# Two operand tensors of TensorE placed elsewhere in SBUF: chunks 16 bytes further apart, and a tensor behind the arena

## Chip, cores, metric

One core of one Trainium2 chip runs the whole program. The metric is the device time of one execution in microseconds (us), the median of several; lower is better.

## What is computed

Two transformer blocks, one behind the other, on 256 tokens of width 1024, all in float32. The first block has two layers, each with a SwiGLU, an attention (sliding window with sinks beside a latent attention in layer 0, forgetting attention in layer 1), a second SwiGLU and a gated projection. The second block merges a block attention with a gated spatial mix, attends to a memory of 256 rows, and ends in a retrieval layer over 16,384 experts. Cut to the two parts that bear on the change:

```python
def swiglu(x, w_gate_up, w_down):                 # four times, 1024 -> 2816 -> 1024
    g, u = jnp.split(x @ w_gate_up, 2, axis=-1)
    return (jax.nn.silu(g) * u) @ w_down
...
def peer_ffn(h, w_q, subkeys, w_down, w_up):      # once, 16384 experts
    ...
    a = jax.nn.gelu(jnp.einsum("td,thkd->thk", xc, w_down[e]))
    return jnp.einsum("thk,thkd->td", g * a, w_up[e])
```

## The kernel before

Tokens are in two tiles of 128 (`NT`), the width in eight chunks of 128 (`KC`). Weights stream from HBM in units of 1 MB (`raw`, a ring of three units, each of four blocks of 512 columns). Full float32 accuracy comes from a split: ScalarE rounds a unit to float32r (`w_hi`, line 276) and VectorE keeps the rest (`w_lo`, line 281). The activations are split in the same way, and both halves stand side by side: `x_both` is [128 partitions, 8 chunks, 2 halves, 256 tokens], `a_both` the same with 4 chunks. The views `x_hi`, `x_lo`, `a_hi`, `a_lo` are its halves.

Each product is three matmuls of float32r. There are two ways in which they stand:

- `product` (lines 321, 322, 325) serves all dense layers and the way down in the retrieval layer. The stationary operand, loaded by LDWEIGHTS, is 128 tokens of one chunk of `x_both` or `a_both`; the moving operand is a block of 512 columns of `w_hi` or `w_lo`. `product_part` (lines 2550 to 2552) does the same at the very end, in part with 256 columns.
- `wide_pair` (lines 2177 and 2180) serves the queries and the way up in the retrieval layer. Here the stationary operand is 128 columns of the weights, and the moving operand is a whole chunk of `x_both` or `a_both`, both halves in one run of 512 elements (line 2177), or its first half alone (line 2180). Two chunks go together: two matmuls of 512 columns, then two of 256, called a four below.

```python
for k in (k0, k0 + 1):
    pe.matmul(out[:, :], w_hi[:, s, b, at:at + P], source(k).rearrange("p s t -> p (s t)"), ...)
for k in (k0, k0 + 1):
    last = pe.matmul(out[:, 0:T], w_lo[:, s, b, at:at + P], source(k)[:, 0, :], ...)
```

In the queries `source(k)` is `x_both` for all eight k. In the experts it is `wide_both` (line 2149): chunks 0 to 3 of `x_both`, then the four of `a_both`. A third user is the forget gate (lines 1429 to 1434): its stationary operand is `f_both`, of 32 or 16 columns, its moving operand 256 columns of `x_both`.

ScalarE and VectorE write both tensors: lines 350 and 360 (a chunk at a time), and lines 2530 and 2537 (two chunks in one instruction). Every engine's order is written out by hand, with semaphores between them; nothing in it depends on an address.

**Places.** SBUF tensors lie in a partition in the order in which they are created, each start rounded up to 32 bytes. In the built program `w_hi` starts at byte 41,088 and takes 24,576 bytes, then come `w_lo`, `h` (90,240), `x_both` (98,432), `a_both` (114,816), `mid` (123,008), `gated`, the small tensors, `one_i` (137,664), `f_both` (150,464) and `arena` (152,128, 69,632 bytes). From `w_hi` to `x_both` it is 57,344 bytes, 28 times 2,048, and a chunk of `x_both` or `a_both`, a block of `w_hi` or `w_lo` and a half of `mid` each have 2,048 bytes. So each of these starts a whole number of times 2,048 bytes from `w_hi`, and each 128 columns a multiple of 512 bytes: this is called the grid below. `f_both` (109,376 bytes from `w_hi`) and `arena` (111,040) are off it, by 320 and 448 bytes over a multiple of 512.

Of the kernel before, what the change touches and what calls it, by code (L numbers as in the profile page):

```python
# [7 lines left out]
F32R = mybir.dt.float32r  # L8
# [9 lines left out]
T, D = 256, 1024  # L18
NT, KC = T // P, D // P
# [17 lines left out]
EC = 4  # L37
# [4 lines left out]
EV_WIDTHS = (384, 384, 416)  # L42
EV_COLS = (0, 384, 768, 1184)
BLOCK = 32

# [98 lines left out]
def build(nc, a, stop=None):  # L146
    with ExitStack() as ctx:
        def sb(name, cols, dt=F32):
            return ctx.enter_context(nc.sbuf_tensor(name, [P] + list(cols), dt))
# [22 lines left out]
        raw = sb("raw", [RING, UB, BLK])  # L172
        w_hi, w_lo = sb("w_hi", [RING, UB, BLK], F32R), sb("w_lo", [RING, UB, BLK], F32R)
        h = sb("h", [NT, D])
        x_both, a_both = sb("x_both", [KC, 2, T], F32R), sb("a_both", [EC, 2, T], F32R)
        x_hi, x_lo = x_both[:, :, 0, :], x_both[:, :, 1, :]
        a_hi, a_lo = a_both[:, :, 0, :], a_both[:, :, 1, :]
        mid = sb("mid", [NT, BLK])
        gated = sb("gated", [EC, T])
        gains, consts = sb("gains_sb", [N_GAINS]), sb("consts_sb", [N_CONSTS])  # L180
# [4 lines left out]
        f_hi, f_lo = f_both[:, :, 0, :], f_both[:, :, 1, :]  # L185
        stat = sb("stat", [5, 2 * HEADS_C])
        arena = sb("arena", [17408])
        banks = ctx.enter_context(nc.psum_tensor("banks", [P, 8, BLK], F32))
        bank = [banks[:, b, :] for b in range(8)]
        ACC, BACK = (0, 1, 2, 3), 6  # L190
# [461 lines left out]
        def vector_back(dve, key, c, quarters):  # L652

            b = c % 2
            for q in quarters:
                if q == 0:
                    dve.wait_ge(*dve_done["mid", key, c, 1])
                rows = slice(q * BLOCK, (q + 1) * BLOCK)
                src = mid[rows, :, b * FC:(b + 1) * FC].rearrange("p t (f o j) -> p t f o j", f=2, j=BLOCK)
                for o in range(P // BLOCK):  # L660
                    dst = turned[o * BLOCK:(o + 1) * BLOCK, b, :, :].rearrange("p f (t o i) -> p t f o i", t=NT, i=BLOCK)
                    last = dve.transpose(dst[:, :, :, q, :], src[:, :, :, o, :])  # L662
# [2333 lines left out]
```

## Time and profile before

| | |
|---|---|
| runs | 2036.25, 2036.39, 2036.99 us, median 2036.39 |
| span of the profiled execution | 2034.3 us |
| its own time | not listed beside the span; the median is 2.1 us above the span |
| TensorE (matmuls) busy | 2021.4 us, 99% |
| weight loads busy | 1698.9 us, 84%, beside the matmuls |
| VectorE, ScalarE, GpSimd busy | 1545.4, 1076.5, 23.3 us |
| bytes moved by DMA | 433.76 MB, mean 213 GB/s |

The span is the time from the first instruction to the last in one profiled execution. A matmul's record is longer than the distance to the next one, because matmuls overlap in the array; what a matmul costs is the distance from its start to the start of the next.

### The profile page before, as it was taken

How to read it: one execution, taken by the hardware profiler on the slowest of the kernel's cores; microseconds unless marked ns; L12 is line 12 of the kernel's file. 1: busy time of each engine (PE TensorE's matmuls, PEld its weight loads, DVE VectorE, ACT ScalarE, POOL GpSimd, SP SyncE). 2: the span in 40 equal slices, each digit the busy share in tenths (PEclk: the TensorE clock that was granted, in tenths of full speed). 3: DMA queues.
4: the chain of work that ended last, by engine and by line, in shares of the span. 5: the costliest groups of instructions: out<-in, count | busy, mean ns of one | idle time of the engine just before them, and what ended most of it. 6: DMA issues, size and time to landing. Idle time of an engine off the chain costs nothing.

```text
span 2034.3 us, 26355 instructions
## 1 busy us (share of the span) xinstructions
PE 2021.4 (99%) x10387; PEld 1698.9 (84%) x10387; DVE 1545.4 (76%) x2466; ACT 1076.5 (53%) x1332; POOL 23.3 (1%) x38
## 2 busy tenths in 40 slices
PE   9999999999999999999999999999999999999998
PEld 7888788888888887888888888888888888888887
DVE  7886778876977566887676756999989857677675
ACT  6445664446444556444557556556566654444443
POOL 0000000000000000000000000000000000000000
PEclk9999999999999999999999999999999999999999
DMA  7654345554555442555554535466799998777773
GB/s 266 226 197 168 137 163 192 201 189 168 206 189 204 149 162 110 202 191 189 189 207 148 184 126 206 161 234 230 236 293 287 298 333 319 305 303 280 281 287 114
DMA packets 97033, 433.76 MB, mean 213 GB/s; under 512 B 7728, under 2 KB 41152, under 8 KB 52496
## 3 DMA queue, kind: packets, MB, share of 16 engines
q1 hardware_dynamic: 95584, 426.51, 59.0%
q0 software_dynamic: 1328, 5.58, 0.8%
q8 instruction: 83, 1.36, 0.3%
q14 instruction: 38, 0.31, 0.0%
HBM read 397.46 MB, written 34.60 MB: 212 GB/s over the span
## 4 chain that ended last, share of the span: by engine, by line
PE 96%; DVE 2%; ACT 1%; issue 0%; DMA 0%; SPq 0%; POOLq 0%; POOL 0%; DVEq 0%; ACTq 0%
PE banks L321 23%; PE banks L325 23%; PE banks L322 23%; PE banks L2177 13%; PE banks L2180 7%; PE banks L328 3%; PE banks L2400 1%; PE banks L981 1%; PE banks L1016 1%; DVE w_lo L281 1%; DVE arena L662 0%; PE banks L507 0%; PE banks L2240 0%; DMA raw<-in_w 0%; PE banks L406 0%
## 5 line engine op out<-in xcount | busy, mean ns | idle before, releaser
L281 DVE TENSOR_TENSOR w_lo<-raw,w_hi 128x2048 fp32r<-128x2048 f32 x334 | 763.9, 2290 | 269.7 <-ACT w_hi L276 268.0
L276 ACT ACTIVATE w_hi<-raw 128x2048 fp32r<-128x2048 f32 x335 | 640.4, 1914 | 471.6 <-PE banks L325 457.0
L321 PE MATMUL banks<-w_hi,x_both 128*128 128x512 f32 (+2 forms) x1488 | 581.0, 390 | 0.4 <-DVE mid L743 0.2
L325 PE MATMUL banks<-w_hi,x_both 128*128 128x512 f32 (+2 forms) x1488 | 577.0, 388 | 0.0
L322 PE MATMUL banks<-w_lo,x_both 128*128 128x512 f32 (+2 forms) x1488 | 576.8, 388 | 0.0
L321 PEld LDWEIGHTS banks<-w_hi,x_both 128*128 128x128 f32 x1488 | 279.3, 188 | 58.1 <-issue 1.1
L325 PEld LDWEIGHTS banks<-w_hi,x_both 128*128 128x128 f32 x1488 | 279.3, 188 | 56.9
L322 PEld LDWEIGHTS banks<-w_lo,x_both 128*128 128x128 f32 x1488 | 279.5, 188 | 54.8
L321 PE MATMUL banks<-w_hi,a_both 128*128 128x512 f32 x608 | 239.8, 394 | 0.3 <-DVE a_both L1103 0.2
L325 PE MATMUL banks<-w_hi,a_both 128*128 128x512 f32 x608 | 236.8, 390 | 0.0
L322 PE MATMUL banks<-w_lo,a_both 128*128 128x512 f32 x608 | 236.8, 389 | 0.0
L2177 PE MATMUL banks<-x_both,w_hi 128*128 128x512 f32 x640 | 203.7, 400 | 0.0
L662 DVE STREAM_TRANSPOSE arena<-mid 32x128 f32<-32x128 f32 x640 | 193.5, 302 | 9.1
L2177 PE MATMUL banks<-a_both,w_hi 128*128 128x512 f32 x512 | 160.8, 395 | 0.0
L2180 PEld LDWEIGHTS banks<-x_both,w_lo 128*128 128x128 f32 x640 | 120.2, 188 | 28.4
L321 PEld LDWEIGHTS banks<-w_hi,a_both 128*128 128x128 f32 x608 | 114.1, 188 | 25.1 <-issue 1.5
L325 PEld LDWEIGHTS banks<-w_hi,a_both 128*128 128x128 f32 x608 | 114.1, 188 | 24.2
L322 PEld LDWEIGHTS banks<-w_lo,a_both 128*128 128x128 f32 x608 | 114.2, 188 | 22.6
L2180 PE MATMUL banks<-x_both,w_lo 128*128 128x256 f32 x640 | 126.0, 278 | 0.0
L2180 PEld LDWEIGHTS banks<-a_both,w_lo 128*128 128x128 f32 x512 | 96.2, 188 | 22.7
L2180 PE MATMUL banks<-a_both,w_lo 128*128 128x256 f32 x512 | 100.6, 278 | 0.0
L2177 PEld LDWEIGHTS banks<-x_both,w_hi 128*128 128x128 f32 x640 | 97.4, 189 | 0.1
(238 smaller groups left out, 1669.7 us busy)
## 6 DMA issues: line engine op xcount, KB each, us to landing
raw<-in_w SPq DMA_DIRECT2D x337, 1024.0 KB, 4.8
parked_t<-arena SPq DMA_DIRECT2D x32, 512.0 KB, 9.6
arena<-parked_t SPq DMA_DIRECT2D x8, 2048.0 KB, 10.5
arena<-parked_a SPq DMA_DIRECT2D x32, 512.0 KB, 5.9
parked_a<-one_i SPq DMA_DIRECT2D x21, 512.0 KB, 7.6
parked_a<-mid SPq DMA_DIRECT2D x11, 512.0 KB, 8.1
raw<-in_w SPq DMA_DIRECT2D x12, 256.0 KB, 7.1
one_i<-in_alibi POOLq DMA_DIRECT2D x1, 1024.0 KB, 6.1
```

The source lines that it names most:

```text
L276: act.activation(w_hi[:, u % RING, :, :], raw[:, u % RING, :, :], ACT.Copy).then_inc(*act_done.mark("w_hi", u))
L281: e.tensor_tensor(w_lo[:, u % RING, :, :], raw[:, u % RING, :, :], f32(w_hi[:, u % RING, :, :]), ALU.subtract).then_inc(*dve_done.mark("w_ ...
L321: pe.matmul(out, hi, w_hi[:, s, b, 0:width], start=start, stop=False)
L322: pe.matmul(out, hi, w_lo[:, s, b, 0:width], start=False, stop=False)
L325: return pe.matmul(out, lo, w_hi[:, s, b, 0:width], start=False, stop=stop)
L328: return pe.transpose(out, src, ident[0:src.shape[0], 0:src.shape[0]])
L662: last = dve.transpose(dst[:, :, :, q, :], src[:, :, :, o, :])
L981: last = pe.matmul(bank[b][:, j * nk:(j + 1) * nk], self.q(h0 + j, n), self.k(h0 + j)[:, k0:k0 + nk], start=True, stop=not self.masks)
L1016: last = pe.matmul(out, self.v(rh + j, tiles[i]), self.ext_at(r)[:, (j * len(tiles) + i) * P:(j * len(tiles) + i + 1) * P], start=i == 0, ...
L2177: pe.matmul(out[:, :], w_hi[:, s, b, at:at + P], source(k).rearrange("p s t -> p (s t)"), start=k == 0, stop=False)
L2180: last = pe.matmul(out[:, 0:T], w_lo[:, s, b, at:at + P], source(k)[:, 0, :], start=False, stop=k == KC - 1)
L2400: last = pe.matmul(bank[banks[j // 4]][:, j % 4 * P:(j % 4 + 1) * P], hot_i[:, slot, j // 2, :, j % 2], hot_j[:, slot, 1 + k, j // 2, :, j ...
```

## The change

`x_both` becomes a view of a tensor with rows of 516 elements, of which 512 are used, so a chunk starts 2,064 bytes behind the last one instead of 2,048. `a_both` is created last, behind `arena`. Nothing else is changed: on all five engines the same instructions stand in the same order, with the same shapes.

```diff
+APART = 4
...
-        x_both, a_both = sb("x_both", [KC, 2, T], F32R), sb("a_both", [EC, 2, T], F32R)
-        x_hi, x_lo = x_both[:, :, 0, :], x_both[:, :, 1, :]
-        a_hi, a_lo = a_both[:, :, 0, :], a_both[:, :, 1, :]
+        x_rows = sb("x_both", [KC, 2 * T + APART], F32R)
+        x_both = x_rows[:, :, 0:2 * T].rearrange("p k (s t) -> p k s t", s=2)
...
         arena = sb("arena", [17408])
+        a_both = sb("a_both", [EC, 2, T], F32R)
+        x_hi, x_lo = x_both[:, :, 0, :], x_both[:, :, 1, :]
+        a_hi, a_lo = a_both[:, :, 0, :], a_both[:, :, 1, :]
```

In the built program `x_both` still starts at 98,432; its chunk k is 16 k bytes off the grid. `a_both` starts at 213,696, which is 172,608 bytes from `w_hi`, 576 more than a multiple of 2,048 (64 more than one of 512). All that lies between, from `mid` to `arena`, moves down by 8,192 bytes less 128.

## Rows read from the trace of the kernel before

**Rows 1.** The page: busy time, and the chain that ended last, by engine and line.

```profile
PE 2021.4 (99%) x10387; PEld 1698.9 (84%) x10387; DVE 1545.4 (76%) x2466; ACT 1076.5 (53%) x1332; POOL 23.3 (1%) x38
...
PE 96%; DVE 2%; ACT 1%; issue 0%; DMA 0%; SPq 0%; POOLq 0%; POOL 0%; DVEq 0%; ACTq 0%
```

**Rows 2.** Span and mean granted TensorE clock of the core; PE's waits for DMA.

```profile
core 0: 2034.3 us, clock 0.999
...
PE banks L328 <- DMA consts_sb<-in_consts: 2.8, 1, 2.8
```

**Rows 3.** The page: groups by line; count, busy us, mean ns of a record.

```profile
L321 PE MATMUL banks<-w_hi,x_both 128*128 128x512 f32 (+2 forms) x1488 | 581.0, 390 | 0.4 <-DVE mid L743 0.2
...
L321 PE MATMUL banks<-w_hi,a_both 128*128 128x512 f32 x608 | 239.8, 394 | 0.3 <-DVE a_both L1103 0.2
...
L2177 PE MATMUL banks<-x_both,w_hi 128*128 128x512 f32 x640 | 203.7, 400 | 0.0
...
L2177 PE MATMUL banks<-a_both,w_hi 128*128 128x512 f32 x512 | 160.8, 395 | 0.0
```

**Rows 4.** Timeline of PE in a dense layer: start us, length us, instruction.

```profile
499.66 0.39 PE L321 MATMUL banks<-w_hi,x_both 128*128 128x512 f32 x1
...
511.90 0.39 PE L321 MATMUL banks<-w_hi,x_both 128*128 128x512 f32 x1
```

**Rows 5.** Timeline of PE, experts: fours of chunks 2-3, 4-5, 6-7, 0-1.

```profile
1500.31 0.63 PE L2177 MATMUL banks<-x_both,w_hi 128*128 128x512 f32 x2
1500.78 0.40 PE L2180 MATMUL banks<-x_both,w_lo 128*128 128x256 f32 x2
1501.01 0.63 PE L2177 MATMUL banks<-a_both,w_hi 128*128 128x512 f32 x2
1501.48 0.39 PE L2180 MATMUL banks<-a_both,w_lo 128*128 128x256 f32 x2
...
1502.17 0.40 PE L2180 MATMUL banks<-a_both,w_lo 128*128 128x256 f32 x2
1502.40 0.63 PE L2177 MATMUL banks<-x_both,w_hi 128*128 128x512 f32 x2
1502.87 0.39 PE L2180 MATMUL banks<-x_both,w_lo 128*128 128x256 f32 x2
...
1504.49 0.63 PE L2177 MATMUL banks<-a_both,w_hi 128*128 128x512 f32 x2
```

**Rows 6.** Timeline of PE, queries: second matmul pairs of chunks 0-1 and 2-3.

```profile
1271.81 0.40 PE L2180 MATMUL banks<-x_both,w_lo 128*128 128x256 f32 x2
...
1272.51 0.39 PE L2180 MATMUL banks<-x_both,w_lo 128*128 128x256 f32 x2
```

**Rows 7.** Timeline of PE, last unit: 256 columns, stationary 128 columns.

```profile
2025.97 0.28 PE L2551 MATMUL banks<-w_lo,x_both 128*128 128x256 f32 x1
...
2027.89 0.28 PE L2552 MATMUL banks<-w_hi,x_both 128*128 128x256 f32 x1
```

**Rows 8.** Timeline of PE, forget gate: 256 columns, stationary 32 or 16 columns.

```profile
693.48 0.28 PE L1429 MATMUL banks<-x_both,f_both 128*32 128x256 f32 x1
...
694.61 0.28 PE L1434 MATMUL banks<-x_both,f_both 128*16 128x256 f32 x1
```

**Rows 9.** Timeline of PE, the unsplit product (plain float32): eight matmuls and the next.

```profile
223.83 3.60 PE L507 MATMUL banks<-raw,mid 128*128 128x512 f32 x8
227.26 0.38 PE L981 MATMUL banks<-arena 128*128 128x128 f32 x2
```

**Rows 10.** Weight loads by line: ns min/median/max, first and last start.

```profile
L321 PEld LDWEIGHTS banks<-w_hi,x_both x1488: 186/188/192, 19.2 to 2016.4; 128*128 128x128 f32 x186
...
L507 PEld LDWEIGHTS banks<-raw,mid x24: 188/190/192, 217.6 to 226.4; 128*128 128x128 f32 x24
...
L2240 PEld LDWEIGHTS banks<-arena x64: 187/192/192, 1260.2 to 1302.4; 128*128 128x128 f32 x64
```

**Rows 11.** Groups by form on ACT and DVE, on and off the grid: busy us, mean ns.

```profile
L2530 ACT ACTIVATE x_both<-gated 128x512 fp32r<-128x512 f32 x44 | 25.0, 615 | 0.0
...
L2490 ACT ACTIVATE mid<-banks 128x512 f32<-128x512 f32 x22 | 13.2, 598 | 50.9 <-PE banks L2180 50.9
L1038 ACT ACTIVATE arena<-banks 128x512 f32<-128x512 f32 x10 | 6.0, 597 | 6.8 <-PE banks L328 6.7
```

## The prediction

> **What bounds the kernel.** I read the page's busy times and its chain first: TensorE is busy for 99% of the span, and 96% of the chain that ended last is TensorE's own [rows 1]. Then the clock and PE's waits: it holds full speed (0.999), and its longest wait for a transfer is 2.8 us, once, at the start [rows 2]. So nothing but the pace of the matmuls counts, and that is read from distances between starts in PE's timeline, by kind of matmul, since no instruction is added, removed or moved.
>
> - Dense layers, moving weights, stationary tokens: from 499.66 to 511.90 us there are 54 steps, 226.7 ns each [rows 4]. At the full clock of 2.4 GHz 512 columns take 213.3 ns, so each matmul has 13.4 ns over its columns.
> - Wide fours, moving tokens, stationary weights: from 1500.31 to 1504.49 there are six fours [rows 5], 696.7 ns each. Two matmuls at 226.7 ns would leave 243.3 ns for the two of 256 columns.
> - 256 columns with a full stationary operand: 1.92 us over 16 steps, 120 ns each [rows 7], again 13.3 ns over the columns (106.7 ns). With a stationary operand of 32 or 16 columns it is 1.13 us over 10 steps, 113 ns [rows 8], 6.3 ns over.
> - Plain float32, which streams at half the pace: 3.43 us for eight, 428.8 ns each, 2.1 ns over twice 213.3 [rows 9].
>
> The surplus is thus the same for 512 and for 256 columns, and it shrinks with the stationary operand. It belongs to the weight load, not to the stream.
>
> **The change, part by part.** What changes is at which byte of a partition an operand starts. The question is if any duration depends on that.
>
> *Chunks of x_both, 16 bytes further apart.* They are stationary in 3 x 1488 matmuls of the dense kind and moving in 640 wide ones and as many of 256 columns [rows 3]. Chunk 0 keeps its distance to the weights, chunks 1 to 7 leave the grid by 16 to 112 bytes. Three readings say that the place does not matter. First, the dense distance is 226.7 ns through all chunks, both halves and both token tiles of the stretch, at all the distances between operands that occur. Second, the wide fours do have a small rhythm, and it does not go with the address: in the experts the pair of 256 columns on chunks 0-1 is recorded with 0.39 us and that on chunks 2-3 with 0.40 us, and so on in turn [rows 5], while in the queries, with the same chunks of x_both and the same places in the weight unit, chunks 0-1 have 0.40 us and chunks 2-3 have 0.39 us [rows 6]. If a distance of addresses set it, it could not change sides. It is a beat of the pipeline that starts anew behind each interruption. Third, f_both lies off the grid by 320 bytes over a multiple of 512, and its matmuls are the ones with the small surplus [rows 8]; the surplus per stationary column is no lower than on the grid (6.3 ns for at most 32 columns, 13.4 ns for 128), so that being off the grid neither freed it nor hurt it visibly.
>
> What no row shows is a full-pace stream whose stationary operand of 128 columns is off the grid, so this term is bounded from both sides. Upwards: weight loads on the grid take 190 ns (from mid), off it 192 ns (from arena), both of plain float32 [rows 10]; 2 ns for each affected matmul is the most that these rows allow. Downwards: the whole surplus over the best paced stream, 13.4 less 2.1, is 11.3 ns. I take 0, since the three readings are of the very instructions in question and the 2 ns are within the loads' own spread (188 to 192 ns from mid).
>
> *a_both behind the arena.* It is stationary in 3 x 608 dense matmuls and moving in 512 wide ones and 512 of 256 columns [rows 3], 2848 in all. In before it runs exactly as x_both does: its fours stand in the same 696.7 ns rhythm [rows 5]. Now it is 64 bytes over a multiple of 512 away from the weights. The bounds per matmul are the same, and I take 0 for the same reasons. That it is 98,880 bytes further up can't matter for a reason that a row shows: w_hi and w_lo are 24,576 bytes apart, and both feed the same 226.7 ns.
>
> *All from mid to arena moves down.* Transposes, attention, scatter and the tables keep their distances to each other; only those to the weights change. Transfers keep their rows and sizes, and PE waits for none of them after the start [rows 2].
>
> *ScalarE and VectorE.* The writes of two chunks at once now step by 2,064 bytes. The nearest rows: ScalarE's 128x512 copy from PSUM takes 598 ns into mid, on the grid, and 597 ns into arena, off it [rows 11]. Into x_both from gated it takes 615 ns. Even 10 ns more on these few dozen would be hidden: both engines have a quarter or more of the span idle, and the chain has 2% and 1% of them [rows 1]. Cost 0; should that cover go, 64 pairs of two at 10 ns are 1.3 us.
>
> The sum is 0. Against the profiled execution's span of 2034.3 us that is a span of 2034.3 us; the median of the runs shown stands 2.1 us above the span, and I forecast 2036.4 us.
>
> A rule on the pace stands against "0". The Trainium skill, page "TensorE: Matmul & The Clock Gate", section "Back-to-back issue gap", gives a warm distance of N/2.4 + 2.5 ns, which is 215.8 ns for 512 columns. The plain float32 row agrees with its surplus, the float32r rows are 10.9 ns above. If placement were what keeps them from it, the gain would be that of rival B. The same skill, page "SBUF — State Buffer", section "Who interferes with whom", gives PE two independent read ports, one for the moving operand and one for the weight load; by that the two could not disturb each other at any distance, and the sum would stay 0. No run here shows the ports.
>
> **The rivals.** A difference of 0.2%, 4.1 us, is about what a measurement of this kernel can tell from none.
>
> *A: only the wide fours get smoother.* If the skew lets the moving chunks stream without the extra beat, a four would go from 696.7 ns to 2 x 226.7 + 2 x 113 = 679.4 ns. There are (640 + 512) / 2 = 576 fours; 17.3 ns each is 10.0 us, to 2026.4 us. With the 120 ns of the last unit instead, a four would take 693.4 ns, and 576 x 3.3 ns = 1.9 us, no change that can be told. For it: these are the only matmuls with the touched tensors as moving operand, and they are slower than the dense ones. Against it: the beat changes sides between equal addresses [rows 5, 6].
>
> *B: weight read and stream collide on the grid.* Then the surplus of every matmul off the grid falls to 2.1 ns: (7/8 x 4464 + 1824) = 5730 x 11.3 ns = 64.7 us in the dense layers. Seven eighths of the 320 x_both fours and all 256 of a_both make 536, each going from 696.7 to 2 x 215.4 + 2 x 108.8 = 648.4 ns, 25.9 us. Together 90.6 us, to 1945.8 us. For it: the surplus exists, and goes with the size of the weight load and with the pace. Against it: f_both, already off the grid, still pays 6.3 ns for a quarter of the columns or less.
>
> *C: loads off the grid are longer, and that is not hidden.* The price is the 2 ns of arena over mid [rows 10]. On a_both's 2848 matmuls it is 5.7 us, to 2042.1 us; if chunks 1 to 7 of x_both pay too, 7/8 x (4464 + 1280) = 5026 more, 15.7 us in all, to 2052.1 us. It decides from the point where the matmul after the load has to start later for it. A load of 188 ns overlaps a distance of 226.7 ns, so a longer record need not show; but a fixed surplus that goes with the load suggests that part of it is on the path. From 1.4 ns on, on a_both alone, it could be told. Against it: 190 and 192 ns are medians within one spread.
>
> That the change doesn't do what it says can be left aside: the built program has the new addresses.
>
> **How the numbers follow.** No change: 0.71. A: 0.11, of which the small version falls under no change. B: 0.03, with 0.01 for some other gain. C: 0.14. So faster 0.15, same 0.71, slower 0.14. No change alone holds 2036.4 give or take 1.5 us and not 8 in 10. A and C's a_both case are about equally likely, so the range takes in both: 2026 to 2043 us. B and the full C stay out.
>
> **What would show it.** Right: 226.7 ns between dense matmuls on x_both and on a_both, 696.7 ns a four, 120 and 113 ns for the 256 columns, loads of 188 ns, TensorE busy within 2 us of 2021.4. A shows as a shorter distance in the fours with 226.7 ns unchanged; B as 215 ns in every dense layer but for chunk 0; C as 188 going to 190 or more on a_both and a distance grown by as much. A gain or loss in which no distance between matmuls has moved would prove my reading of the bound wrong.

## The result, and the profile after

The changed kernel takes 2069.43 us in the median (2068.88 to 2070.03, 4 runs) against 2036.56 us for the kernel before, measured with it (2036.25 to 2036.99). The ratio is 1.0161, with a 95% interval of 1.0149 to 1.0173: 32.9 us slower, outside the range given. The profiled execution took 2069.60 us, with a span of 2067.8 us; the same 1.8 to 2.1 us lie around the span.

The page after the change, busy times and the groups that answer to [rows 1, 3]; lines are three further down:

```profile
PE 2055.1 (99%) x10387; PEld 1703.3 (82%) x10387; DVE 1546.0 (75%) x2466; ACT 1077.4 (52%) x1332; POOL 23.2 (1%) x38
...
L324 PE MATMUL banks<-w_hi,x_both 128*128 128x512 f32 (+2 forms) x1488 | 588.0, 395 | 0.2
...
L324 PE MATMUL banks<-w_hi,a_both 128*128 128x512 f32 x608 | 243.6, 401 | 0.3 <-DVE a_both L1106 0.2
...
L2180 PE MATMUL banks<-x_both,w_hi 128*128 128x512 f32 x640 | 203.2, 398 | 0.0
...
L2180 PE MATMUL banks<-a_both,w_hi 128*128 128x512 f32 x512 | 159.8, 393 | 0.0
```

VectorE and ScalarE are busy for as long as before, to within 1 us, and no wait of PE grew: its busy time grew by 33.7 us. The mean records of the dense matmuls are 5 to 7 ns longer (390 to 395, 394 to 401), those of the wide ones are 2 ns shorter. PE's timeline in the same dense layer as [rows 4] (start us, length us):

```profile
500.18 0.40 PE L324 MATMUL banks<-w_hi,x_both 128*128 128x512 f32 x1
...
506.94 0.39 PE L328 MATMUL banks<-w_hi,x_both 128*128 128x512 f32 x1
```

These are 29 steps, 6.76 us, 233.1 ns each instead of 226.7 ns. Clock and waits are unchanged (answering [rows 2]), and so are the weight loads, 188 ns on either tensor (answering [rows 10]):

```profile
core 0: 2067.8 us, clock 1.000
```

```profile
PE banks L331 <- DMA consts_sb<-in_consts: 2.8, 1, 2.8
```

```profile
L324 PEld LDWEIGHTS banks<-w_hi,x_both x1488: 186/188/193, 20.5 to 2049.8; 128*128 128x128 f32 x186
L324 PEld LDWEIGHTS banks<-w_hi,a_both x608: 186/188/190, 42.7 to 2038.6; 128*128 128x128 f32 x152
```

Adding up the distances from each matmul's start to the next one's, in both traces, gives where the span's 33.5 us went:

| matmuls | before us | after us | difference |
|---|---|---|---|
| dense on x_both, 512 columns, x4320 | 985.8 | 1006.6 | +20.8 |
| first unit of the program, x48 | 11.2 | 12.2 | +1.0 |
| dense on a_both, x1824 | 417.9 | 428.7 | +10.8 |
| fours with x_both, x320 | 225.9 | 226.8 | +0.9 |
| fours with a_both, x256 | 178.4 | 177.8 | -0.6 |

That is 32.9 of 33.5 us, nearly all of it on the matmuls whose stationary operand was moved. Below, "distance" alone means this time from start to start; "off the grid by n" is the number of bytes between operand and streamed weights over a multiple of 256, the period that the runs gave. The theory going in (P): what counts is where the stationary operand lies in relation to the streamed one. The other letters (L, S, A0 and those that follow) name the rivals, each in the expectation where it first stands.

### The profile page after: what moved, and what is told of

It is laid out like the page before. It is cut to its first block, busy times and chain, and to the rows that moved or that the text cites. A ratio compares the mean times of both kernels' runs of the same rounds, so it can differ in the third digit from the quotient of the medians.

```text
span 2067.8 us, 26355 instructions
## 1 busy us (share of the span) xinstructions
PE 2055.1 (99%) x10387; PEld 1703.3 (82%) x10387; DVE 1546.0 (75%) x2466; ACT 1077.4 (52%) x1332; POOL 23.2 (1%) x38
## 4 chain that ended last, share of the span: by engine, by line
PE 98%; DVE 1%; ACT 0%; issue 0%; DMA 0%; SPq 0%; POOLq 0%; POOL 0%; DVEq 0%
PE banks L324 24%; PE banks L325 23%; PE banks L328 23%; PE banks L2180 13%; PE banks L2183 7%; PE banks L331 3%; PE banks L2403 1%; PE banks L984 1%; PE banks L1019 1%; PE banks L510 0%; PE banks L2243 0%; PE banks L409 0%; PE banks L412 0%; DMA h<-in_x 0%; PE banks L415 0%
## 5 line engine op out<-in xcount | busy, mean ns | idle before, releaser
L324 PE MATMUL banks<-w_hi,x_both 128*128 128x512 f32 (+2 forms) x1488 | 588.0, 395 | 0.2
L325 PE MATMUL banks<-w_lo,x_both 128*128 128x512 f32 (+2 forms) x1488 | 583.5, 392 | 0.0
L328 PE MATMUL banks<-w_hi,x_both 128*128 128x512 f32 (+2 forms) x1488 | 583.3, 392 | 0.0
L324 PE MATMUL banks<-w_hi,a_both 128*128 128x512 f32 x608 | 243.6, 401 | 0.3 <-DVE a_both L1106 0.2
L328 PE MATMUL banks<-w_hi,a_both 128*128 128x512 f32 x608 | 240.3, 395 | 0.0
```

The source lines that it names most:

```text
L324: pe.matmul(out, hi, w_hi[:, s, b, 0:width], start=start, stop=False)
L325: pe.matmul(out, hi, w_lo[:, s, b, 0:width], start=False, stop=False)
L328: return pe.matmul(out, lo, w_hi[:, s, b, 0:width], start=False, stop=stop)
```

## Each part alone, and the same parts on the grid

**Only the 16 bytes between chunks.**

```diff
         x_both = x_rows[:, :, 0:2 * T].rearrange("p k (s t) -> p k s t", s=2)
+        between = sb("between", [480])
+        a_both = sb("a_both", [EC, 2, T], F32R)
```

> Only the 16 bytes between the chunks of x_both; a_both stays behind x_both and on the grid (480 unused elements fill up to it). Theory P (what counts is the distance, to within a few hundred bytes, between the stationary operand that is being loaded and the columns that are streaming): the dense matmuls on x_both keep their longer distances (after: 7.3 + 7.2 + 6.4 us more on lines 321, 322, 325, 0.9 us in the first unit), those on a_both go back to 227 ns; about 22 us over before, 2059 us. Rival L (what hurts is that a_both lies far away, behind the arena, or beside nothing): the dense distances on x_both would be as before, 2036.5 us. Rival S (the step of 2,064 bytes hurts writes or multi-chunk operands and PE waits for them): 2059 us too, but with PE's dense distances at 227 ns and the loss in waits.

**Only a_both moved.** (`APART = 0`, and 128 unused bytes that keep a_both's byte.)

```diff
-APART = 4
+APART = 0
...
+        between = sb("between", [32])
```

> Only a_both behind the arena, at the same byte as in the change; x_both's chunks at 2,048 bytes again (128 unused bytes behind it). Theory P: dense distances on a_both 233 ns as in the change, on x_both 227 ns; the a_both part of the loss is 3.9 + 3.8 + 3.1 us dense less 0.6 us in the fours, so 2047 us. Rival L: the same on a_both. Together with the other part it should add up to the 33 us of the change if the two parts are independent.

**a_both behind the arena, on the grid.** The last kernel with 1,472 more unused bytes.

```diff
+        behind = sb("behind", [368])
         a_both = sb("a_both", [EC, 2, T], F32R)
```

> As the run with a_both alone moved, but 1,472 unused bytes ahead of a_both, so that it lies behind the arena and yet a whole number of times 2,048 bytes from w_hi. Theory P: all dense distances 227 ns, 2036.5 us, no change. Rival L (place far away): 233 ns on a_both as before this padding, 2047 us.

**All of the kernel before, 64 bytes later.**

```diff
+        ahead = sb("ahead", [16])
         raw = sb("raw", [RING, UB, BLK])
```

> The kernel before with 64 unused bytes ahead of everything, so every operand starts 64 bytes later, and all distances between operands are kept. Theory P: 227 ns everywhere, 2036.5 us. Rival A0 (the operand's own address counts, a start at 64 bytes over the old one is slow as a_both's is in the change): dense distances 233 ns on both tensors, some 35 us more, 2071 us.

Measured together, against 2036.81 us for the kernel before:

| kernel | us | ratio (95%) | dense distance on x_both, a_both |
|---|---|---|---|
| x_both's chunks apart | 2062.13 | 1.0126 (1.0109 to 1.0143) | 229.5 to 233.7 ns by chunk, 228.1 |
| a_both moved | 2051.16 | 1.0072 (1.0055 to 1.0088) | 227.3, 233.3 |
| a_both behind, on the grid | 2036.60 | 1.0000 (0.9990 to 1.0009) | 227.0, 227.1 |
| all shifted by 64 | 2036.63 | 0.9999 (0.9989 to 1.0009) | 227.0, 227.1 |

(Distances here are means from the starts in each trace, leaving out those over 300 ns; the kernel before has 227.0 and 227.2 by the same count.) The kernel with a_both moved, the one line by tensor, as ns min/median/max of a record:

```profile
L325 PE MATMUL banks<-w_hi,x_both x1488: 334/389/577, 20.3 to 2031.8; 128*128 128x512 f32 x180, 128*128 128x384 f32 x4, 128*128 128x416 f32 x2
...
L325 PE MATMUL banks<-w_hi,a_both x608: 393/398/504, 42.1 to 2020.9; 128*128 128x512 f32 x152
```

And the one with a_both behind the arena and on the grid:

```profile
L326 PE MATMUL banks<-w_hi,a_both x608: 389/389/504, 41.6 to 2005.9; 128*128 128x512 f32 x152
```

A record of 389 ns goes with a distance of 227 ns, 394 with 233 and 398 with 236. With a_both alone moved, the slow matmuls are those whose own operand was moved, and 1,472 bytes of padding take the whole loss on a_both away with the tensor still behind the arena. So it is neither the place nor the neighbourhood (L falls), and no start address in itself (A0 falls), but the relation between the operands. S falls too: no wait of PE grew.

A rival of another kind is that the moved operand meets the other engines' reads and writes of SBUF, or the transfers, and not PE's own stream. The trace of the kernel with a_both moved speaks against it. 39 of its dense matmuls on a_both ran, from 230 ns ahead of their start to the start of the next one, with no instruction on ScalarE, VectorE or GpSimd: 233.3 ns on average, as all of them. 408 ran with no DMA packet under way: 233.2 ns.

The two parts cost 25.3 and 14.4 us, 39.7 us in sum, against 32.9 us together. The missing 6.8 us lie in what each part does to matmuls that it does not touch: in the fours (with x_both apart alone, the fours on the untouched a_both take 702.6 ns instead of 697.1; with a_both moved alone, its own take 703.6 and x_both's 699.3; with both parts 694.7 on a_both; all of these without the 34 fours on x_both that stand behind an interruption) and in the dense ones on a_both next to skewed ones, 228.1 ns with x_both apart alone. So the time of a matmul depends on the matmuls around it too.

## Which distances are slow

Four kernels, one execution each, give the chunks of x_both 32 placements and a_both four. The edits are the step (`APART = 32`, then 4), an unused tensor ahead of x_both, and one between it and a_both.

> Chunks of x_both 128 bytes further apart (distances to the weights 0, 128, ... 896 bytes off the grid), a_both 256 bytes off the grid for all its chunks. Theory P with a short period (64 bytes or less would be contradicted already, since 64 is slow; a period of 128 bytes): 227 ns on all chunks, 2036.5 us. P with a period of 256: chunks 0, 2, 4, 6 and a_both at 227 ns, chunks 1, 3, 5, 7 slower, up to 235 ns, some 15 us in all. P with a period of 512: only chunks 0 and 4 at 227 ns, a_both slow too, some 30 us. Rival N (any distance off the grid is slow, however the distance): all but chunk 0 near 233 ns, over 35 us.

> x_both starts 128 bytes off the grid and steps by 16 (128 to 240), a_both 32 bytes off. With a period of 128 bytes the dense distances by chunk repeat those of the change: 229.5, 231, 232, 233, 234, 229.5, 234, 233 ns. With a longer period they differ. a_both: about 232 ns, as chunk 2 of x_both in the change.

> x_both 256 to 368 bytes off the grid in steps of 16, a_both 128 bytes off. With a period of 256 (or 128) bytes: as in the change by chunk, about 25 us over before. Otherwise the eight values show what the distance does, and whether any place is faster than the grid's 227 ns (by the surplus over the columns the most that could be had is 11 ns).

> x_both 384 to 496 bytes off the grid in steps of 16, a_both 448 bytes off (64 bytes short of a multiple of 512). Theory P says that only the distance counts; whether it is symmetric (448 like 64, so 233 ns) or whether a load that lies just ahead of the stream is better or worse is open. A place faster than 227 ns, if there is one, would be among these or the last runs' ones.

They took 2056.80, 2068.88, 2071.73 and 2064.51 us, beside 2036.64 us for the kernel before. Mean dense distance by bytes off the grid, from all kernels so far; where there are two numbers they are the least and the most of the chunks (of either tensor) at that place:

| bytes (mod 256) | 0 | 16 | 32 | 48 | 64 | 80 | 96 | 112 |
|---|---|---|---|---|---|---|---|---|
| ns | 227.0 | 231.0 to 231.1 | 231.6 to 233.4 | 232.6 to 232.8 | 233.0 to 233.4 | 230.4 to 230.9 | 233.7 to 233.8 | 232.3 to 232.6 |

| bytes (mod 256) | 128 | 144 | 160 | 176 | 192 | 208 | 224 | 240 |
|---|---|---|---|---|---|---|---|---|
| ns | 231.6 to 233.9 | 232.5 to 232.6 | 232.8 | 229.8 to 230.5 | 229.0 to 231.5 | 232.2 | 232.6 | 232.3 to 232.6 |

The 227.0 ns at 0 is that of kernels wholly on the grid. In the run with steps of 128 bytes a_both at 256 had 227.4 to 228.5 ns, chunks at 0, 256, 512 and 768 had 230.2 to 230.8 ns, and those at 128, 384, 640 and 896 had 231.6 to 233.5 ns: 128 is slow and 256 is not. The eight chunks at 256 to 368 bytes took what those at 0 to 112 took in the change to 0.4 ns, but for the first of them, 230.4 against 229.3 ns. So the period is 256 bytes, and an on-grid chunk between off-grid ones pays 2 to 4 ns for its neighbours. The rival of "any distance is alike" (N) falls with 80, 176 and 192. It falls most cleanly on a_both, whose chunks all lie alike: 233.0 ns at 32, 233.4 at 64, 233.2 at 128 and 229.2 at 448, that is 192. So it is not symmetric either. No chunk was faster than on the grid, though of the three matmuls of a product on a_both at 192 the first took 226.5 ns, the third 231.7.

**Steps of 256 bytes** (`APART = 64`, a_both right behind):

> Chunks of x_both 256 bytes further apart, a_both right behind on the grid. Theory P, with the period of 256 bytes that the scan gave: all dense distances 227 ns, 2036.5 us, no change, though no two chunks lie a multiple of 2,048 bytes apart. Rival Q (consecutive chunks must lie a whole number of 512, 1,024 or 2,048 bytes apart): some 15 us or more over before, at chunks 1, 3, 5, 7.

2036.77 against 2036.49 us, ratio 1.0001 (0.9992 to 1.0011), 226.8 to 227.3 ns for every chunk. So chunks may be as far apart as one likes in steps of 256 bytes, and Q falls.

**Steps of 4 bytes** (`APART = 1`):

> Chunks of x_both 4 bytes (one element) further apart, so chunk k lies 4 k bytes off the grid; a_both 32 bytes off. Theory P in the form that only whole 16-byte pieces count: chunks 0 to 3 as chunk 0 of the change (227 to 229.5 ns), chunks 4 to 7 as its chunk 1 (231 ns). If starting inside a 16-byte piece costs something of its own, chunks 1, 2, 3, 5, 6, 7 are slower than chunks 0 and 4. The matmuls on a_both: 233 ns, as at 32 bytes in the scan.

2069.30 us, in one execution. Chunks 0 to 7 had 230.8, 232.4, 231.7, 231.4, 231.9, 231.4, 231.5 and 233.7 ns, and a_both 233.2 ns, as expected. Four bytes off are already slow, in no order that whole 16-byte pieces would give, but chunk 0, on the grid, isn't at 227 ns in this company either. What starting inside a piece of 16 bytes costs by itself isn't told apart.

## Which pair of operands it is

**w_lo alone shifted.**

```diff
-        w_hi, w_lo = sb("w_hi", [RING, UB, BLK], F32R), sb("w_lo", [RING, UB, BLK], F32R)
+        w_hi = sb("w_hi", [RING, UB, BLK], F32R)
+        ahead = sb("ahead", [48])
+        w_lo = sb("w_lo", [RING, UB, BLK], F32R)
+        behind = sb("behind", [464])
```

> Placement of before, but w_lo 192 bytes further (64 short of a multiple of 256), so that the distance from w_lo to x_both and a_both is 64 bytes over the grid and that of w_hi is unchanged; 1,856 unused bytes behind w_lo keep the rest. Theory P: only the distances of line 322, which streams w_lo, go to 233 ns, lines 321 and 325 stay at 227 ns; 2048 matmuls by 6 ns, 12 us, 2049 us, give or take what the fours do. Rival X (the place of x_both or a_both against something other than the streamed weights, such as raw, h or consts): no change.

2048.12 us, in one execution as the next two: the total is as expected, its place is not. The distances on x_both are 229.4, 229.4 and 228.5 ns on lines 324, 325 and 328 (321, 322, 325 of before), not 227, 233 and 227. X, which had no change, falls.

**The halves of x_both 64 bytes apart.** The wide matmul takes its operand as two runs of 256.

```diff
-        x_both, a_both = sb("x_both", [KC, 2, T], F32R), sb("a_both", [EC, 2, T], F32R)
+        x_rows = sb("x_both", [KC, 2 * T + 64], F32R)
+        x_both = x_rows[:, :, 0:2 * T + 32].rearrange("p k (s t) -> p k s t", s=2)[:, :, :, 0:T]
+        a_both = sb("a_both", [EC, 2, T], F32R)
```

> In x_both the second half (x_lo) of each chunk starts 64 bytes later, chunks 2,304 bytes apart (on the 256-byte grid); a_both untouched. The wide matmul reads the two halves as two runs of 256. Line 322 loads x_lo's weights for line 325 while w_lo streams; line 325 itself then runs with x_lo as its stationary operand, while the next x_hi is loaded. Theory P (the load for the next matmul against the stream of this one): of the dense distances on x_both, line 322's go to about 233 ns, lines 321 and 325 stay near 227 ns. Rival O (the matmul's own stationary operand against its own stream): line 325's go to 233 ns, 321 and 322 stay. In both 1440 by 6 ns, 9 us, so some 2045 us.

2055.10 us. The three lines of `product` on x_both, ns min/median/max of a record:

```profile
L323 PE MATMUL banks<-w_hi,x_both x1488: 334/389/583, 20.1 to 2035.5; 128*128 128x512 f32 x180, 128*128 128x384 f32 x4, 128*128 128x416 f32 x2
...
L324 PE MATMUL banks<-w_lo,x_both x1488: 335/392/398, 20.3 to 2035.7; 128*128 128x512 f32 x180, 128*128 128x384 f32 x4, 128*128 128x416 f32 x2
...
L327 PE MATMUL banks<-w_hi,x_both x1488: 331/397/401, 20.5 to 2036.0; 128*128 128x512 f32 x180, 128*128 128x384 f32 x4, 128*128 128x416 f32 x2
```

The distances are 228.5, 229.2 and 235.4 ns. The largest part falls on the matmul with x_lo as its own stationary operand, where O has it, and not on the one beside whose stream x_lo is loaded. But the loss is 18.6 us, twice the 9 us that both P and O gave.

**Both low parts 64 bytes further**, so that x_lo is again in step with w_lo (the last edit, and 16 and 496 unused elements around w_lo):

> As the run with x_lo 64 bytes further, and w_lo 64 bytes further too. On x_both line 322 then streams w_lo (64) while it loads x_lo (64): distance 0; lines 321 and 325 stream w_hi (0) and load x_hi (0): distance 0. If the load for the next matmul against the present stream is what counts (P), all three are at 227 ns on x_both. If the matmul's own stationary operand against its own stream counts (O), line 322 (x_hi, w_lo) and line 325 (x_lo, w_hi) are both slow, 233 ns or more. If it is the step from one load to the next (or from one stream to the next) that counts (R), line 325 stays near 235 ns as in the last run. On a_both, which has no gap, line 322 loads on the grid against w_lo at 64: some 229 ns in all three, as in the run with w_lo shifted.

2065.82 us, and 232.1, 231.3 and 230.3 ns on x_both: all three are slow. P in its narrow form (only load against present stream) would have 227 ns three times, O 227 ns on the first, R 235 ns on the third. All three fail. a_both, which has no gap, was expected at 229 ns and took 231.9, 232.1 and 232.1 ns:

```profile
L327 PE MATMUL banks<-w_lo,a_both x608: 387/395/398, 43.1 to 2035.4; 128*128 128x512 f32 x152
```

The three matmuls of a product together, over the 680.9 ns (x_both) or 681.4 ns (a_both) of the kernel before; the middle columns say how far off the grid each one's own stationary operand is from its own stream:

| run, tensor | 321 | 322 | 325 | ns over before |
|---|---|---|---|---|
| a_both moved, a_both | 64 | 64 | 64 | 18.5 |
| from 256 in steps of 16, a_both | 128 | 128 | 128 | 18.1 |
| from 384 in steps of 16, a_both | 192 | 192 | 192 | 6.1 |
| w_lo shifted, x_both | 0 | 64 | 0 | 6.4 |
| halves apart, x_both | 0 | 0 | 64 | 12.1 |
| both low parts, x_both | 0 | 192 | 64 | 12.8 |
| both low parts, a_both | 0 | 192 | 0 | 14.7 |

No fixed price for each distance gives this: 192 on one line of three costs more than 192 on all three. R alone, the step between successive operands, has no way to explain the first three rows, where no such step was changed; that steps have a part in the last four isn't excluded. What is shown is that the cost goes with how stationary and streamed operands lie to each other, and that it spreads over neighbouring matmuls; which load counts against which stream, and what a mixture costs, stays open.

## Can the fours have it better

With w_lo shifted by 192 bytes the fours took 690 to 692 ns in the median instead of 697. Only the 72 units that the fours use were given that shift:

```diff
-        w_hi, w_lo = sb("w_hi", [RING, UB, BLK], F32R), sb("w_lo", [RING, UB, BLK], F32R)
+        w_hi, lo_rows = sb("w_hi", [RING, UB, BLK], F32R), sb("w_lo", [RING, UB * BLK + 64], F32R)
+        w_lo, w_lo_wide = [lo_rows[:, :, o:o + UB * BLK].rearrange("p r (b n) -> p r b n", b=UB) for o in (0, 48)]
...
+                lo = w_lo_wide if 0 <= u - first["peer_q"] < 2 * (4 + NKEYS // EC) else w_lo
-                e.tensor_tensor(w_lo[:, u % RING, :, :], raw[:, u % RING, :, :], f32(w_hi[:, u % RING, :, :]),
+                e.tensor_tensor(lo[:, u % RING, :, :], raw[:, u % RING, :, :], f32(w_hi[:, u % RING, :, :]),
...
-                last = pe.matmul(out[:, 0:T], w_lo[:, s, b, at:at + P], source(k)[:, 0, :], ...)
+                last = pe.matmul(out[:, 0:T], w_lo_wide[:, s, b, at:at + P], source(k)[:, 0, :], ...)
```

> Everything on the grid as before, but the 72 units that the fours use keep their w_lo 192 bytes further in its slot (slots 256 bytes larger), all other units on the grid. In the run with w_lo shifted for all, the fours took 690 to 692 ns in the median instead of 697, at the cost of the dense ones. Here dense distances should be 227 ns and the fours 690 to 695 ns: 576 x 2 to 7 ns, 1 to 4 us faster than before, 2032.5 to 2035.5 us. If the fours' gain came from their neighbours and not from their own w_lo, no change.

> The same with 64 bytes instead of 192: if only being off the grid helps the fours, the same gain; if the distance counts and is not symmetric, another number, by the scan up to 705 ns a four, 4 us slower.

With 192 bytes: 2035.48 against 2036.87 us, ratio 0.9994 (0.9984 to 1.0003), so not told from no change by the times. The trace shows the fours themselves, six of them between these starts, 4.16 us or 693.3 ns each, where [rows 5] have 696.7:

```profile
1500.18 0.62 PE L2179 MATMUL banks<-a_both,w_hi 128*128 128x512 f32 x2
...
1504.34 1.09 PE L2402 MATMUL banks<-arena 128*128 128x128 f16 x16
```

The means are 694.2 ns on x_both and 695.4 ns on a_both, against 697.1. Summed over all fours that is 0.8 and 0.4 us, 1.2 us in all; the medians differ by 1.4 us. With 64 bytes the kernel took 2038.73 us in its one execution and the fours 700.5 and 701.2 ns, 2.1 us more in all. So here too the place has a part in the pace, with another best place than in the dense matmuls. No version measured is faster than the kernel before by more than its measurement can tell.

## Why the prediction was wrong

- **What bounds the kernel** held. PE is busy for 99% again, no wait grew, and the whole loss is in distances between matmuls. That is also why 5 to 6 ns on some 6,150 dense matmuls come out in full.
- **"Three readings say that the place does not matter"** is the step that failed. From it came the term of 0 for both tensors. The first reading, 226.7 ns at all distances between operands that occur, was true and worth nothing: every distance between these operands was a multiple of 512 bytes, so it was one sample of a quantity with a period of 256. The runs showed 231.9 ns on x_both and 233.4 ns on a_both in its place, and 227.0 ns again as soon as both were on a grid of 256 bytes.
- The second reading, the beat that changes sides between equal addresses, showed that what stands ahead of a matmul has a part in its time, and the runs agree (an untouched a_both at 228.1 ns, fours at 702.6). It doesn't follow that addresses have no part in it: with w_lo of these units shifted by 192 bytes the median four took 690 and 692 ns, by 64 bytes 700.
- The third, f_both, has its chunks 64 and 192 bytes off the grid in turn, but with loads of 32 columns at most. Its 16 matmuls took 114.2 ns on average in the kernel before and 117.2 ns in the change, which moved f_both by 128 bytes and skewed the chunks that it meets. With a_both alone moved, which moves f_both but leaves the skew out, they took 116.3 ns. So its place seems to count too, by 2 to 3 ns, but 16 matmuls are few, and the surplus per column could not show it: the trace held no f_both on the grid to compare with.
- **The bounds** of the term were taken from the wrong row. Upwards 2 ns came from the length of weight loads, which did not move (188 ns). Measured: +6.2 ns on a_both, 229.3 to 233.8 ns by chunk on x_both. The trace of the kernel before had a nearer one, the wide matmuls of the same shape. Their median record is 396 ns long, against 389 for a dense one, and on a_both they stand 233 ns apart instead of 227:

```profile
L321 PE MATMUL banks<-w_hi,a_both x608: 389/389/504, 41.2 to 2005.8; 128*128 128x512 f32 x152
...
L2177 PE MATMUL banks<-a_both,w_hi x512: 389/396/398, 1291.1 to 1679.6; 128*128 128x512 f32 x171
```

As an upper bound, these 6 ns on 6,144 dense matmuls are 37 us.
- **Rival C** had the sign and the tensors right and the mechanism wrong: loads did not get longer (188 ns), and its full case, 2052.1 us, is half of the loss. **A** was right that placement can smooth the fours, by some 1.2 us at best here and not by this change. **B** was the opposite of the truth: the grid is the fast place, and the surplus of 13.4 ns stays.
- The Trainium skill's two independent read ports of PE (page "SBUF — State Buffer", section "Who interferes with whom") were read as "no distance can matter". No run shows the ports; the runs show that where the one operand lies against the other costs up to 8 ns a matmul (235.4 against 227.2 ns on the third line with the halves apart). The rule on the pace (page "TensorE: Matmul & The Clock Gate", section "Back-to-back issue gap") isn't met by the float32r matmuls at any of the places tried; the best stayed at 227.0 ns for 512 columns. The section calls the formula that of a single, isolated matmul and gives another figure for a stream, which the prediction left out; at some 131 ns for 512 columns that one isn't met here either.

## What to carry to other kernels

Before concluding from a trace that a quantity doesn't matter, ask how many values of it the trace holds; here a kernel laid out in blocks of 2,048 bytes held one. In a float32r kernel bound by TensorE, with matmuls of 512 columns like these, keep every stationary operand a multiple of 256 bytes from the streamed one, and pad small tensors so that those behind them stay there: creating one tensor in another place cost 14 us, and 1,472 unused bytes gave it back. The sign is cheap to see: the median record of a matmul by line and tensor, here 389 ns on the grid and 394 or 398 off it.

## What the runs showed of the hardware that was not expected

- The distance of back-to-back float32r matmuls (512 columns, 128 stationary columns) depends on the bytes between stationary and streamed operand with a period of 256: 227.0 ns at 0, 229 to 234 ns elsewhere where all matmuls of a tensor are moved alike or in steps, 233.4 ns at 64 and 229.2 ns at 192. Where only one operand of a product is moved, the same distance can cost more or less (table above).
- Shifting all operands alike by 64 bytes changes nothing (2036.63 us), nor does a distance of 174,080 bytes instead of 73,728 (2036.60 us).
- An operand off the grid also slows matmuls around it that are on the grid, by 1 to 4 ns.
- Plain float32 matmuls did not show it. The one such pair whose distance changed, `raw` streamed past `mid`, went from 0 to 128 bytes off the grid in the change and kept 429 ns for 512 and 322.5 ns for 384 columns, in all 24 matmuls; 192 bytes off, in the run from 384 in steps of 16, they took the same. The transposes of `h` kept 109 ns in the median. The float16 scatter has both operands in the arena, so its distances never changed and it can't tell.
